# mLSTM output products of a two-layer backbone: plain fp32 matmuls replaced by three passes over high and low parts

## What is computed

```python
s   = einsum('bhid,bhjd->bhij', q, k) * exp(log_d - m_row)      # weighted scores, queries i, keys j
num = einsum('bhij,bhje->bhie', s, v)                           # <- the products that are changed
h   = num / maximum(abs(den), exp(-m_row))                      # den: sum of s over the keys
hs  = layernorm_nobias(h_forward + h_backward, mh_norm)         # then (hs + skip * xc) * silu(z)
```

## Time and profile before

| | |
|---|---|
| Median of 3 runs | 2371.76 us (2371.61 to 2375.91) |
| The profiled execution | 2372.35 us, span 2370.6 us, mean granted clock 0.983 |
| TensorE matmul busy | 2278.3 us (96%), 11867 instructions |
| VectorE busy | 1370.7 us (58%) |
| ScalarE busy | 905.5 us (38%) |
| GpSimd busy | 1050.3 us (44%) |

### The profile page before, as it was taken

How to read it: one execution, slowest core, us unless ns; L and a number is a source line. 1 busy time by engine, 2 the same in 40 slices (tenths; PEclk the granted TensorE clock), 3 DMA queues, 4 the chain that set the end, 5 groups by cost and what they waited for, 6 DMA issues and landing times.

```text
span 2370.6 us, 32621 instructions
## 1 busy us (share of the span) xinstructions
PE 2278.3 (96%) x11867; PEld 1968.3 (83%) x11867; DVE 1370.7 (58%) x1749; ACT 905.5 (38%) x1979; POOL 1050.3 (44%) x815
## 2 busy tenths in 40 slices
PE   7999999999879999999999999999999999999998
PEld 5999999998536999999999998976555568888887
DVE  5995787764666356857857456654568654111113
ACT  5215435433894256756746252232221213101002
POOL 3353234334541445534544434355133045766664
PEclk9999999999998999999999999999999999999999
DMA  7953334254540234534534423454233212333332
GB/s 269 303 170 114 105 109 128 96 178 139 181 129 21 70 98 121 147 105 124 148 102 131 82 74 116 134 166 143 60 109 102 67 45 82 105 98 97 98 95 82
DMA packets 392725, 281.07 MB, mean 119 GB/s; under 512 B 33443, under 2 KB 357821, under 8 KB 392605
## 3 DMA queue, kind: packets, MB, share of 16 engines
q1 hardware_dynamic: 333420, 200.46, 28.6%
q10 hardware_dynamic: 59184, 78.99, 9.8%
HBM read 237.34 MB, written 42.07 MB: 118 GB/s over the span
## 4 chain that ended last, share of the span: by engine, by line
PE 63%; DVE 4%; ACT 2%; DMA 1%; issue 1%; POOL 1%; ACTq 0%; DVEq 0%; SPq 0%; POOLq 0%
PE PS L960 46%; PE PS L1644 3%; PE PS L1473 3%; PE PS L1485 3%; PE PS L1596 2%; PE PS L1290 1%; PE PS L1545 1%; DMA xmr<-xm_d 1%; DVE xcr L2490 1%; PE PS L1422 0%; PE PS L1564 0%; PE PS L892 0%; PE PS L898 0%; PE PS L1356 0%; PE PS L1409 0%
## 5 line engine op out<-in xcount | busy, mean ns | idle before, releaser
L960 PE MATMUL PS<-act_hi,w_hi 128*128 128x384 f32 (+1 forms) x1824 | 641.2, 352 | 11.1 <-DVE act_lo L2465 4.0
L960 PE MATMUL PS<-act_hi,w_lo 128*128 128x384 f32 (+1 forms) x1824 | 632.7, 347 | 0.0
L960 PE MATMUL PS<-act_lo,w_hi 128*128 128x384 f32 (+1 forms) x1824 | 629.5, 347 | 0.0
L742 POOL TENSOR_TENSOR w_hi<-w_raw,ones 128x128 fp32r<-128x128 f32 x232 | 130.3, 562 | 1076.6 <-DMA w_raw<-in_ffn_w 406.9
L745 POOL TENSOR_TENSOR w_lo<-w_raw,w_hi 128x1024 fp32r<-128x1024 f32 (+1 forms) x232 | 559.1, 2410 | 19.3
L960 PEld LDWEIGHTS PS<-act_hi,w_hi 128*128 128x128 f32 x1824 | 345.0, 189 | 35.8 <-issue 17.5
L960 PEld LDWEIGHTS PS<-act_lo,w_hi 128*128 128x128 f32 x1824 | 345.0, 189 | 15.2 <-issue 1.2
L960 PEld LDWEIGHTS PS<-act_hi,w_lo 128*128 128x128 f32 x1824 | 344.6, 189 | 13.7
L2107 ACT ACTIVATE fprod<-mf_ring,cs 128x128 f32<-128x128 f32 x896 | 267.9, 388 | 26.6 <-DVE mf_acc L2405 26.6
L2405 DVE TENSOR_REDUCE mf_acc<-fprod 128x128 f32<-128x1024 f32 x112 | 224.7, 2019 | 86.0 <-ACT fprod L2107 86.0
L743 POOL TENSOR_SCALAR w_hi<-w_raw 128x896 fp32r<-128x896 f32 (+1 forms) x232 | 232.4, 1002 | 0.0
(11 more groups left out here) (373 smaller groups left out, 3680.5 us busy)
## 6 DMA issues: line engine op xcount, KB each, us to landing
w_raw<-in_ffn_w SPq DMA_DIRECT2D x120, 512.0 KB, 4.0
mf_ring<-in_w_mod SPq DMA_DIRECT2D x56, 512.0 KB, 3.8
w_raw<-in_a_w_in SPq DMA_DIRECT2D x44, 512.0 KB, 4.1
proj<-stage ACTq DMA_DIRECT2D x44, 384.0 KB, 4.2
w_raw<-in_b_w_up SPq DMA_DIRECT2D x32, 512.0 KB, 4.5
m_ring<-in_w_mod SPq DMA_DIRECT2D x12, 1024.0 KB, 9.2
rows<-g_d SPq DMA_DIRECT2D x16, 768.0 KB
m_raw<-in_w_mod SPq DMA_DIRECT2D x4, 2048.0 KB, 11.6
```

The source lines that it names most:

```text
L742: pool.tensor_tensor(w_hi[:, s, 0], w_raw[:, s, 0], ones[:], ALU.mult)
L960: last = pe.matmul(to[:, c0:c1], w[:, s, k, :], x[:, k, c0:c1], start=k == 0 and w is w_hi and x is hi, stop=k == kt - 1 and w is w_lo)
```

## The change

The weights and the centred values are each split into a high part (fp32r) and the rest, and each product becomes three fp32r products: values high by weights high, values low by weights high, values high by weights low, four banks at a time. `Wf_hi` takes the place of `Wb`, `Wf_lo` that of `Wf` itself; the parts of the values lie in `vparts`, two buffers (blocks of keys alternate) in the place of `hh`. ScalarE makes the high parts (`value_high`, `weight_high`), GpSimd the low values (`low_values`), VectorE the low weights (`weight_low`). Five semaphores are used again with new base counts.

```diff
+        vparts = sb("vparts", [P, 2, 2, LAT], F32R, offset=51200)
+        Wf_hi = nc.alloc_sbuf_tensor_at("Wf_hi", [P, 6, LAT], F32R, offset=Wb_at)
+        Wf_lo = sb("Wf_lo", [P, 6, LAT], F32R, offset=38912)
@@ gpsimd
+                def low_values(h, chunks):
+                    for i in chunks:
+                        pool.wait_ge(v_high, V_HIGH0 + 6 * h + i + 1)
+                        pool.tensor_tensor(vparts[:, i % 2, 1], vt[:, KEYS[i]], vparts[:, i % 2, 0].bitcast(F32),
+                                           ALU.subtract).then_inc(v_low, 1)
                 if name == "zm":
                     for j in range(count):
...
                         if j == 11:
                             centred_values(0)
+                            low_values(0, (0, 1))
+                    low_values(0, range(2, 6))
                     continue
                 if name == "mout0":
                     for m in range(count):
                         if m in (1, 4, 7):
-                            masks((m + 2) // 3)
+                            h = (m + 2) // 3
+                            masks(h)
+                            centred_values(h)
+                            low_values(h, (0, 1))
                         split((n0 + m) // RING, m % RING, kt)
-                        if m in (1, 4, 7):
-                            centred_values((m + 2) // 3)
+                        if m in (3, 6):
+                            low_values(m // 3, range(2, 6))
+                    continue
+                if name == "mout1":
+                    for m in range(count):
+                        split((n0 + m) // RING, m % RING, kt)
+                        if m == 1:
+                            low_values(3, range(2, 6))
                     continue
@@ tensor
                 for i, c in enumerate(KEYS):
-                    pe.wait_ge(v_cent, V_CENT0 + 6 * h + i + 1)
-                    pe.wait_ge(pn_done, PN_DONE0 + 6 * h + i + 1)
+                    pe.wait_ge(v_high, V_HIGH0 + 6 * h + i + 1)
+                    pe.wait_ge(wf_high, WF_HIGH0 + 6 * h + i + 1)
                     for t in range(4):
-                        last = pe.matmul(bank(OUT_BANKS[t]), vt[:, c, t * P:t * P + P], Wf[:, c], start=i == 0, stop=i == 5)
+                        pe.matmul(bank(OUT_BANKS[t]), vparts[:, i % 2, 0, t * P:t * P + P], Wf_hi[:, c], start=i == 0, stop=False)
+                    pe.wait_ge(v_low, V_LOW0 + 6 * h + i + 1)
+                    for t in range(4):
+                        pe.matmul(bank(OUT_BANKS[t]), vparts[:, i % 2, 1, t * P:t * P + P], Wf_hi[:, c], start=False, stop=False)
+                    pe.wait_ge(wf_low, WF_LOW0 + 6 * h + i + 1)
+                    for t in range(4):
+                        last = pe.matmul(bank(OUT_BANKS[t]), vparts[:, i % 2, 0, t * P:t * P + P], Wf_lo[:, c], start=False, stop=i == 5)
                         if i == 5:
                             last.then_inc(h_mm, 1)
+                    if i < 5:
+                        last.then_inc(key_mm, 1)
@@ scalar
                 for t in range(4):
+                    if h and t == 2:
+                        weight_high(h - 1, 0)
...
+            def value_high(h, i):
+                act.wait_ge(v_cent, V_CENT0 + 6 * h + i + 1)
+                if i >= 2:
+                    act.wait_ge(key_mm, KEY_MM0 + 5 * h + i - 1)
+                act.activation(vparts[:, i % 2, 0], vt[:, KEYS[i]], ACT.Copy).then_inc(v_high, 1)
+            def weight_high(h, i):
+                act.wait_ge(pn_done, PN_DONE0 + 6 * h + i + 1)
+                act.activation(Wf_hi[:, KEYS[i]], Wf[:, KEYS[i]], ACT.Copy).then_inc(wf_high, 1)
+            value_high(0, 0)
+            value_high(0, 1)
             for h in range(ML_HEADS):
...
+                if h + 1 == ML_HEADS:
+                    weight_high(h, 0)
+                weight_high(h, 1)
+                for i in range(2, 6):
+                    value_high(h, i)
+                    weight_high(h, i)
                 for t in range(4):
-                    act.wait_ge(h_mm, H_MM0 + 4 * h + t + 1)
+                    act.wait_ge(h_mm, H_MM0 + 4 * h + (t + 1 if t < 2 else 4))
                     act.activation(hh[:, t], bank(OUT_BANKS[t]), ACT.Copy).then_inc(h_put, 1)
...
+                if h + 1 < ML_HEADS:
+                    act.wait_ge(act_ready, READY["ml0"] + 4 * h + 4)
+                    value_high(h + 1, 0)
+                    value_high(h + 1, 1)
@@ vector
-                for c in KEYS:
+                def weight_low(i):
+                    c = KEYS[i]
+                    dve.wait_ge(wf_high, WF_HIGH0 + 6 * h + i + 1)
+                    dve.tensor_tensor(Wf_lo[:, c], Wf[:, c], Wf_hi[:, c].bitcast(F32), ALU.subtract).then_inc(wf_low, 1)
+                for i, c in enumerate(KEYS):
...
                     chain(dve.tensor_tensor(Wf[:, c, i0:i1], Wf[:, c, i0:i1], Wb[:, c, i0:i1], ALU.add), pn_done)
+                    if i:
+                        weight_low(i - 1)
+                weight_low(5)
```

More of the change, by code:

```diff
@@ L230, in trunk @@
         zst = sb("zst", [P, 2, LAT])
+        Wb_at = top[0]
         Wb = sb("Wb", [P, 6, LAT])
@@ L535, in trunk @@
         mk_done, bdv_done, den_mm, v_mean = (sem("mh_" + n) for n in ("mk_done", "bdv_done", "den_mm", "v_mean"))
+        v_high, V_HIGH0 = e3_done, 8
+        v_low, V_LOW0 = e4_done, 8
+        wf_high, WF_HIGH0 = a_done, 24
+        wf_low, WF_LOW0 = k2_done, 8
+        key_mm, KEY_MM0 = kd_done, 8
         OUT_BANKS = (6, 7, 4, 5)
```

## The result

The changed kernel takes 2377.25 us (median of 22 runs) against 2371.68 us for the kernel before (22 runs beside it). The ratio is 1.0023, 95% interval 1.0013 to 1.0034: slower by 5.5 us (3.1 to 8.1). That lies inside the range given, 4.6 us above the point, and just over the 4.7 us that I had set as the bound of "no change": it fell among the results above 2376.5 us, to which I had given 0.23. One execution of the changed kernel took 6073.89 us and is left out of the ratio; without it the median is 2377.1. The profiled execution took 2380.66 us with a span of 2378.9, mean granted clock 0.981 (before 2372.35, 2370.6 and 0.983).

What follows compares the result with a forecast made beforehand. TensorE was taken as the bound, with little in hand; 17.2 us off for products against 2.8 + 6.6 + 8.7 = 18.1 on gave 2372.7 us from a median of 2371.76, no change that can be told; range 2361 to 2378.

Steps and rivals of the forecast that it cites:

- Rival B: TensorE falls to its lower clock after four more waits in this stretch: 5.6 us on top, 2378.3 us; chance 0.13.
- The products: TensorE's loop over the keys: 72 fp32r products 0.2275 us apart replace 24 plain ones, saving 4.31 us a head, 17.2 in all.
- Rival D: The loop's products miss the dense tiles' pace because they change bank each time; at 0.25 us apart, 2379.2 us; chance 0.04.
- The copies: ScalarE's copies out of the banks end later, so TensorE's `xmr` wait grows 0.94 us in heads 0 to 2: 2.8 us.
- The loop, block 0: Block 0's low weights come late on VectorE behind GpSimd's split in heads 1 to 3: 6.6 us (0 to 9).
- The low values against the sums: GpSimd's first two low values hold VectorE's sums over the keys, splits the reciprocals, heads 1 to 3: 8.7 us (0 to 11).
- The centring, ScalarE's copies, the moved splits of head 0: Moved centring of heads 1 to 3, ScalarE's high-part copies and head 0's moved split: costed at nothing.
- Rival C: The moved centring holds VectorE's sums of squares, 1.8 us in each of three heads: 5.4 us, 2378.1 us; chance 0.07.
- Rival A: The VectorE and GpSimd collisions mostly miss: holds halved to 7.5 us give 2364.9 us, a fifth of them 2360.4; chance 0.30.

Runs made afterwards that it cites:

- e4: Kernel before with only the 24 plain products a head replaced by 72 fp32r ones on stand-in operands, nothing else added; ratio to before 0.9937.
- e6: e4 with its two product loops exchanged, so the bank changes every third product and not every one; ratio to the kernel before 0.9919.
- e8: e3 with the last block of keys multiplied bank by bank, so the banks end 0.7 us apart; 2357.03 us, ratio to the kernel before 0.9941.
- e2: Changed kernel with GpSimd's low values of blocks 2 to 5 put before the split that stood ahead of them; ratio to the kernel before 0.9995.
- e1: Changed kernel with GpSimd waiting for the denominators' signal before the first two low values of heads 1 to 3; 2364.77 us, ratio to the kernel before 0.9988.
- e7: Kernel before with only the centring of heads 1 to 3 moved ahead of the split of tiles 1, 4 and 7; ratio to before 1.0000.
- e3: Changed kernel with the reorderings of e1 and e2 together, no split between a head's last norm and its loop's end; 2357.95 us, ratio to before 0.9957.
- e9: Kernel before with one idle VectorE instruction added ahead of the denominators' signal in heads 1 to 3; ratio to before 1.0030, 7.1 us slower.
- e5: Changed kernel with GpSimd's low values written as subtraction of a number per partition instead of a tensor; ratio to the kernel before 1.0003.

## Why the prediction was near, and what in it was wrong

The sum was 18.1 us on and 17.2 off. Measured, it is 20.7 on (12.2 idle, 8.5 clock) and 15.0 off. The kind of result and most of the places were right. That the number came within 4.6 us is in part luck: the waits were priced 5.9 us too high, the clock behind them was left out, and the products were priced 2.2 us too high. The result lies nearer to B's number (2378.3) than to the forecast.

- **The products** (17.2 us off). About 15.0. The dense tiles' pace of 0.2275 us held for the form: in e4 the products come every 0.227, and a head saves 4.2 us of the 4.31. On the real operands they come every 0.232, and it saves 3.9 (3.4 in head 3). Rival D had the sign and its price for 0.25; its reason, the change of bank, is refuted by e4, where the bank changes at every product.
- **The copies** (2.8 us on). About 1.6: 1.2 in `xmr` waits and 0.4 in the waits for `vt`. Two of the four copies could start before the end. e6 shows the mechanism, and e8 bears it out in head 1.
- **The loop, block 0** (6.6 us on). The mechanism was right: waits of 1.0, 2.0 and 2.3 us in heads 1, 2 and 3 on VectorE's low weights, with GpSimd's L754 beside VectorE (predicted 1.8, 1.6, 3.2). In heads 2 and 3 they stand at the ninth product, as said. In head 1 the split came one block later and the wait stands in block 1, which I had costed at nothing. As idle time that is 5.3 us. Not in my sum is the clock behind it, 1.7 us in each of heads 2 and 3. e2 takes out the waits and 6.6 us.
- **The low values against the sums** (8.7 us on, with the splits against the reciprocals). The first sum was predicted at 1.7 to 2 us and took 1.5 and 1.7; the waits are 1.9, 0.4 and 4.0 us in the three heads, 5.5 more than before. The clock took 5.1 more there, so the place cost 10.6 in this profile; e1, which takes these waits out, gains 8.3. The reciprocals were held as predicted (one spread operand of 2.77 us at 1744.15, one of 2.52 at 1820.56), but TensorE never waited for them; its own tile ahead of them was late by the lower clock, which may be why.
- **The centring, ScalarE's copies, the moved splits of head 0** (nothing). Right: e7, and no row of waits names them. Rival C falls.
- **Rival B, the clock**, was the mechanism that I priced too low. I counted 1.4 us a fall, from six products at the lower level behind the 0.8 us wait of head 3, and four falls, 5.6 us, and gave it 0.13 because one wait of 2.7 us had passed without a fall. The trace shows 8.5 us, all executions 11.1. The slices of the kernel before held the better price, 1.7 us a fall, and so a sign that I did not read: head 1 had a fall with no wait at all, behind the 16 tiny products.
- **Rival A** had 0.30. None of the collisions missed in heads 1 and 3; in head 2 the slack ate most of one. A's number, 2364.9, lies near e1's 2364.77 and well above e3's 2357.95: what it took as luck can be had by order.

So what the centre lacked is its waits' second price. With holds alone the sum would have been -15.0 + 12.2 = -2.8, and over all executions the time without the lost clock did fall, by 4.2 us.

## What to carry to other kernels

Price a wait of TensorE as its length and, possibly, time at the lower level behind it: here 18.1 us of forecast stalls were 12.2 of idle time and 8.5 of clock. Take the clock from many executions, for one profile can miss it (e9) or show too much. Before work is moved to GpSimd, look for the VectorE instructions with two SBUF operands that run beside it on the path, and order the list so that they don't meet: the same instructions in another order turned +5.5 us into -10.2. A product change should be measured by itself first: it tells what there is to win (here 15 us) before its supporting work is judged.

## What the runs showed that I had not expected

- GpSimd's subtraction of a number per partition lets VectorE in (0.69 us in a 3.39 us pair), at a price of 1.6 to 1.7 us for 512 columns instead of 1.25 (2.50 us for two in e3, undisturbed).
- fp32r products of one shape come every 0.227 us in a dense tile and in the loop of e4 and e6, and every 0.232 in the changed kernel's loop, at full granted clock in all.
- The clock's loss is not a function of the wait alone: a wait of 0.65 us (e5, head 1) was followed by 3.4 us of loss, one of 0.73 (e9, head 1) and none at all (before, head 1) by 1.7, one of 2.7 us (before, head 3) by none, one of 2.9 us in the same place of e2 by 3.4. Losses came in steps of about 1.7 us. What decides between them stays open.
